# One decoder step on one core: squares taken in pairs, key groups and weight splits moved, and each chunk's products run one accumulator bank after the other

## The reference, cut to what matters

```python
def rmsnorm(x, g):
    xf = x.astype(jnp.float32)
    y = xf * lax.rsqrt(jnp.mean(xf * xf, axis=-1, keepdims=True) + EPS)
    return (y * g.astype(jnp.float32)).astype(x.dtype)

def ffn_half(x, g_pre, g_post, wi, wo):
    return x + 0.5 * rmsnorm(swiglu(rmsnorm(x, g_pre), wi, wo), g_post)

for i in range(DEPTH):                       # DEPTH = 2, D_MODEL = 1024, D_FF = 2816
    xp = ffn_half(xp, g[0], g[1], ffn1_wi[i], ffn1_wo[i])
    hp = rmsnorm(xp, g[2])
    yp = ab_mixer(hp, ...) if i % 2 == 0 else c_mixer(hp, ...)
    xp = xp + rmsnorm(yp, g[3])
    xp = ffn_half(xp, g[4], g[5], ffn2_wi[i], ffn2_wo[i])
    xp = xp + (p_prompt[i] @ ple_w_pe[i]) * jax.nn.sigmoid(rmsnorm(xp, g[6]) @ ple_w_pg[i])
```

## Time and profile before

| What | Value |
|---|---|
| Runs | 2132.02 us, median of 3 (2131.34 to 2139.12) |
| The profiled execution | 2124.92 us; its span in the trace 2123.1 us |
| TensorE busy | 2094.1 us (99%), 17060 products |
| VectorE, ScalarE, GpSimd busy | 1133.2 us (53%), 712.7 us (34%), 33.5 us (2%) |
| Granted TensorE clock, mean | 0.997 of 2.4 GHz |
| Chain that ended last | PE 85%, DVE 10%, ACT 2% |

### The profile page before, as it was taken

One profiled execution on the slowest core, in us unless ns is written; L12 is line 12 of the kernel. 1 busy time (PEld: TensorE's weight loads), 2 busy tenths in 40 slices (PEclk: granted clock), 3 DMA queues, 4 the chain that ended last, 5 costly groups with the idle time before them and its releaser, 6 DMA issues.

```text
span 2123.1 us, 37973 instructions
## 1 busy us (share of the span) xinstructions
PE 2094.1 (99%) x17060; PEld 2057.1 (97%) x17060; DVE 1133.2 (53%) x1545; ACT 712.7 (34%) x926; POOL 33.5 (2%) x68
## 2 busy tenths in 40 slices
PE   8999999999999999999999999999999999999998
PEld 8999999998879999999999999999998999999998
DVE  6433244855766754234587343244888854323467
ACT  5221122422344422112354222123477432212243
POOL 0000000011010000000000000000000000000000
PEclk9999999999999999999999999999999999999999
DMA  5222222233132222222232222222222132232222
GB/s 173 95 82 87 98 97 80 81 121 120 60 121 80 80 100 90 91 100 82 79 108 100 80 97 88 95 100 80 79 84 101 60 120 83 87 100 90 100 90 81
DMA packets 33633, 198.57 MB, mean 94 GB/s; under 512 B 4648, under 2 KB 4936, under 8 KB 15552
## 3 DMA queue, kind: packets, MB, share of 16 engines
q1 hardware_dynamic: 29520, 183.87, 24.7%
q0 software_dynamic: 3952, 12.28, 1.7%
HBM read 191.68 MB, written 4.46 MB: 92 GB/s over the span
## 4 chain that ended last, share of the span: by engine, by line
PE 85%; DVE 10%; ACT 2%; issue 1%; DMA 1%; POOLq 0%; DVEq 0%; POOL 0%; ACTq 0%
PE acc L1729 69%; PE acc L1834 9%; DVE w_lo L1022 2%; DVE t L1135 2%; PE acc L1770 1%; DVE x L1142 1%; DVE act_lo L1148 1%; PE acc L2034 1%; DVE rs_post L1130 1%; PE acc L2104 1%; DVE xsum L1157 1%; PE acc L1914 1%; DMA raw<-in_weights 1%; PE acc L1968 1%; PE acc L1989 1%
## 5 line engine op out<-in xcount | busy, mean ns | idle before, releaser
L1729 PE MATMUL acc<-act_hi,w_hi 128*128 128x260 f32 x3072 | 621.6, 284 | 0.0
L1729 PE MATMUL acc<-act_hi,w_lo 128*128 128x260 f32 x3072 | 617.5, 282 | 0.0
L1729 PE MATMUL acc<-act_lo,w_hi 128*128 128x260 f32 x3072 | 617.0, 282 | 0.0
L1729 PEld LDWEIGHTS acc<-act_hi,w_hi 128*128 128x128 f32 x3072 | 472.6, 188 | 1.7 <-issue 1.0
L1729 PEld LDWEIGHTS acc<-act_hi,w_lo 128*128 128x128 f32 x3072 | 472.3, 188 | 0.4
L1729 PEld LDWEIGHTS acc<-act_lo,w_hi 128*128 128x128 f32 x3072 | 471.6, 188 | 0.5
L620 ACT ACTIVATE w_hi<-raw 128x2048 fp32r<-128x2048 f32 (+2 forms) x179 | 323.8, 1809 | 277.0 <-DMA raw<-in_weights 276.9
L1022 DVE TENSOR_TENSOR w_lo<-raw,w_hi 128x2048 fp32r<-128x2048 f32 (+2 forms) x179 | 387.6, 2165 | 43.0 <-ACT w_hi L620 42.8
L1267 DVE TENSOR_TENSOR gu<-acc,rs_pre 128x520 f32<-128x520 f32 x164 | 114.3, 698 | 439.4 <-PE acc L1729 439.3
L745 ACT ACTIVATE hid_hi<-gu 128x520 fp32r<-128x520 f32 x86 | 55.0, 639 | 476.5 <-DVE gu L1287 476.5
L1729 PE MATMUL acc<-hid_hi,w_hi 128*128 128x260 f32 x1024 | 206.3, 283 | 0.2
(11 more groups left out here) (287 smaller groups left out, 2148.5 us busy)
## 6 DMA issues: line engine op xcount, KB each, us to landing
raw<-in_weights SPq DMA_DIRECT2D x138, 1024.0 KB, 4.8
raw<-in_weights SPq DMA_DIRECT2D x32, 896.0 KB, 4.6
ring<-in_k_pages POOLq DMA_DIRECT2D x16, 256.0 KB, 4.7
ring<-in_v_pages POOLq DMA_DIRECT2D x16, 256.0 KB, 3.6
raw<-in_weights SPq DMA_DIRECT2D x12, 256.0 KB, 5.3
x<-in_x SPq DMA_DIRECT2D x8, 260.0 KB, 6.6
out_y<-x SPq DMA_DIRECT2D x8, 260.0 KB, 2.0
raw<-in_weights SPq DMA_DIRECT2D x4, 512.0 KB, 3.4
```

Of the source, the lines that this page charges most:

```text
L1729: ins = nc.tensor.matmul(a[0:width, half, 0:HALF], w[slot][:, at:at + width], m[:, half * HALF:(half + 1) * HALF], start=first and n == 0, ...
```

## The change

Four edits. (1) `chunk` runs the three products of one half, all into one bank, and then the three of the other half; the low weights come second instead of third. (2) In `begin`, the squares of two chunks are one instruction of 520 columns and added as such, with one add at the end that folds the two sides (`fold_sum`); VectorE's reciprocal for `pre0` and the drain behind it stand one chunk earlier, the drain of `first1.0` one chunk later, and ScalarE takes the root of `pre0` ahead of its half-1 parts. (3) In the attention, key groups 1, 2 and 3 stand in tiles c0, c1 and c2 (before: v3, x0 and c1), the rows of values behind c0 (before: inside the first head's scores), `decay_sums` at head 2 (before: head 1), and the last head's transposes inside tile b3. (4) In the recurrence, the splits at `i5` and `i7` stand earlier, and the weights of the last output pair (`HALVED`) are split and waited for in two halves.

```diff
 def head_jobs(h):
-    return [["c0", "dec_s2", "x0"], ["dec_s3", "c1", "x1"], ["c2", "x2", "dec_t"], ["dec_p", "c3", "dec_o0", "x3"],
-            ["dec_o1", "b0"], ["dec_o2", "b1"], ["dec_o3", "b2"], ["b3"]][h]
+    return [["dec_s1", "c0", "vt0", "vt2", "x0"], ["dec_s2", "c1", "x1"], ["dec_s3", "c2", "x2", "dec_t"], ["dec_p", "c3", "dec_o0", "x3"],
+            ["dec_o1", "b0"], ["dec_o2", "b1"], ["dec_o3", "b2"], ["pt7.0", "pt7.2", "b3"]][h]
...
+HALVED = PLAN.unit[f"{S_C}.out6"]
...
+                    at = 0
+                    if n == HALVED:
+
+                        at = size // 2
+                        nc.scalar.activation(w_hi[n % SLOTS][:, 0:at], raw(n, at), ACT.Copy).then_inc(half_hi, 1)
...
-                for c in range(KC):
-                    square_half(s, 0, c)
-                    if c == 4:
+                for n in range(4):
+                    square_two(s, 0, n)
+                    if n == 2:
                         root(f"{s}.post1", rs_post, 1)
                 done(f"{s}.first0.0")
+                root(f"{s}.pre0", rs_pre, 0)
                 for c in range(KC):
                     high_half(s, 1, c)
-                    if c == 2:
-                        root(f"{s}.pre0", rs_pre, 0)
...
                 roots(range(0, 4))
+                done(f"{s}.i5")
                 gelus(range(0, 4))
-                done(f"{s}.i5")
...
+            def add_two(s, half, n):
+
+                dve.wait_ge(xsq_ready, square_count(s, 4 * half + n))
+                if n > 1:
+                    dve.wait_ge(xsum_added, added_count(s, 4 * half + n - 1))
+                nc.vector.tensor_tensor(xsum[:, :], xsum[:, :], pair_square(n)[:, :], ALU.add).then_inc(xsum_added, 1)
+
+            def fold_sum(s, half):
+
+                dve.wait_ge(xsum_added, added_count(s, 4 * half + 3))
+                nc.vector.tensor_tensor(cols(xsum, 0), cols(xsum, 0), cols(xsum, 1), ALU.add).then_inc(xsum_added, 1)
...
-                    if c == 3:
+                    if c == 2:
                         invert(f"{s}.pre0", rs_pre, 0)
                         if s == S_AB + 1:
                             dve.wait_ge(stored, 16 * 5)
                         first_drain(s, 0, 0)
-                    if c == 5:
+                    if c == 6:
                         first_drain(s, 1, 0)
...
-                    if h == 1:
+                    if h == 2:
                         decay_sums()
-                    if h == 2:
                         decode_softmax()
...
                 for c in range(4):
                     mixed(c)
+                done(f"{s}.i7")
                 gates(7)
                 mixed_lo(0)
                 mixed_lo(1)
-                done(f"{s}.i7")
...
-                for n, (w, m) in enumerate(((w_hi, hi), (w_hi, lo), (w_lo, hi))):
-                    for half in range(2):
+                for half in range(2):
+                    for n, (w, m) in enumerate(((w_hi, hi), (w_lo, hi), (w_hi, lo))):
...
-                wait_unit(unit)
+                if unit == HALVED:
+                    pe.wait_ge(half_lo, 1)
+                else:
+                    wait_unit(unit)
                 accs = claim(J[name])
                 for c in range(KC):
+                    if unit == HALVED and c == KC // 2:
+                        wait_unit(unit)
...
                     for m in B_TILES.get(h, []):
-                        column_tile(f"b{m}", f"b{m // 2 * 2}", m % 2, with_values(h - 3) if h < MIX_HEAD else None)
+                        column_tile(f"b{m}", f"b{m // 2 * 2}", m % 2, with_values(h - 3) if h < MIX_HEAD else
+                                    lambda c: transposes(MIX_HEAD) if c == 5 else None)
```

More of the change, by code:

```diff
@@ L218, in ab @@
             pl.add_job(f"{s}.v{m}", f"{s}.v{m}")
-            pl.add_job(f"{s}.dec_s{m // 2}")
+            if m == 0:
+                pl.add_job(f"{s}.dec_s0")
             pl.add_job(f"{s}.v{m + 1}", f"{s}.v{m}")
-        for j in ("cq", "ck0", "s0.0", "vt0", "s0.2", "vt2"):
+        for j in ("cq", "ck0", "s0.0", "s0.2"):
             pl.add_job(f"{s}.{j}")
@@ L405, in both, with pair_square @@
             return cols(ap, half).unsqueeze(1).broadcast_to([P, 2, HALF])
-        def half_square(half, c):
-            return cols(xsum, half) if c == 0 else cols(xsq[c // 2 % 2], c % 2)
+        def pair_square(n):
+            return xsum if n == 0 else xsq[n % 2]
         def acc_of(name):
@@ L492, in act_count, with square_count, added_count @@
             return sum(2 * KC if n % 4 else KC for n in range(s)) + KC * half + c + 1
-        def added_count(s, half, c):
-            return sum(2 * (KC - 1) if n % 4 else KC - 1 for n in range(s)) + (KC - 1) * half + c
+        def square_count(s, n):
+            return KC * s + n + 1
+        def added_count(s, n):
+            return sum(KC if i % 4 else KC - 1 for i in range(s)) + n
         def ysum_count(s, n):
@@ L678, in high_half, with square_two @@
                                      scale=pre_gain(s, c)).then_inc(acth_ready, 1)
-            def square_half(s, half, c):
-                if c > 4:
-                    act.wait_ge(xsum_added, added_count(s, half, c - 4))
-                elif half and c:
-                    act.wait_ge(xsum_added, added_count(s, 0, KC - 1))
-                nc.scalar.activation(half_square(half, c), cols(x[:, c, :], half), ACT.Square).then_inc(xsq_ready, 1)
+            def square_two(s, half, n):
+                if n == 3:
+                    act.wait_ge(xsum_added, added_count(s, 4 * half + 1))
+                elif half and n:
+                    act.wait_ge(xsum_added, added_count(s, 4))
+                nc.scalar.activation(two(pair_square(n)[:, :]), half_of(x[:, 2 * n:2 * n + 2, :], half), ACT.Square)\
+                    .then_inc(xsq_ready, 1)
             def first_taps(s, c):
@@ L722, in begin @@
                     nc.scalar.activation(p_hi[:, :, :], p_raw[:, :, :], ACT.Copy).then_inc(ph_ready, 1)
-                for c in range(KC):
-                    square_half(s, 1, c)
+                for n in range(4):
+                    square_two(s, 1, n)
                 root(f"{s}.pre1", rs_pre, 1)
@@ L1223, in begin @@
                 done(f"{s - 1}.out67.1")
-                for c in range(1, 4):
-                    add_half(s, 0, c)
+                for n in range(1, 3):
+                    add_two(s, 0, n)
                 invert(f"{s}.post1", rs_post, 1)
-                for c in range(4, KC):
-                    add_half(s, 0, c)
+                add_two(s, 0, 3)
+                fold_sum(s, 0)
                 done(f"{s}.first0.0")
@@ L1248, in begin @@
                 first_drain(s, 2, 0)
-                for c in range(1, KC):
-                    add_half(s, 1, c)
+                for n in range(1, 4):
+                    add_two(s, 1, n)
+                fold_sum(s, 1)
                 if s % 4 == 3:
@@ L2063, in decode_probs, with transposes @@
                     ins.then_inc(acc_ready, 1)
+                def transposes(h):
+                    pe.wait_ge(probs_ready, QB * (h + 1))
+                    for kb in range(QB):
+                        if kb % 2 == 0:
+                            a = claim(J[f"{s}.pt{h}.{kb}"])
+                        for qb in range(kb, QB):
+                            ins = nc.tensor.transpose(a[:, kb % 2, qb * P:(qb + 1) * P],
+                                                      sc[:, qb, kb * P:(kb + 1) * P], ident)
+                        if kb % 2:
+                            ins.then_inc(acc_ready, 1)
                 decay_column()
```

74 lines of the change are left out of this document (34 added, 40 removed).

## The result

The changed kernel takes 2116.9 us (median of 6 runs, 2114.6 to 2119.6) against 2130.7 us for before (6 runs, 2124.4 to 2139.1): ratio 0.9933, 95% interval 0.9913 to 0.9953, 0.7% less. The two profiled executions, 2124.92 and 2116.38 us, lie 8.5 us apart, the very sum of the prediction. That is luck: its terms are off by up to 2 us each and cancel, and the medians lie 13.8 us apart. Both have to be explained.

What follows compares the result with a forecast made beforehand. TensorE bounds the kernel, busy 2094.1 of 2123.1 us: its product pace and its waits. Terms +2.0 - 4.3 - 2.0 - 5.1 + 1.3 - 0.4 = -8.5 us off the median 2132.02 gave 2123.5; own range 2118 to 2128, overall 2098 to 2139.

Steps and rivals of the forecast that it cites:

- edit 1, order: `chunk`: weights change more often over 12,288 products, costing 2.0 us; adds into one bank taken as no effect.
- edit 2, six begins: `begin`: 1.64 us of TensorE waiting becomes 0.92, a gain of 0.7, six times: 4.3 us.
- edit 4, recurrence: Last output pair: halves shorten the 1.9 us wait for `w_lo`, gain 2.0 us; moved splits at `i5` and `i7` gain 0.
- edit 3, waits: Attention: `decay_sums` at head 2 loses 1.3 us; around b3 1.4 gained, 1.0 lost, net 0.4 gained.
- edit 3, clock: Attention, first heads: the 10.24 us stretch at 1.2 GHz goes, gaining 5.1 us.
- Every sign that the prediction named: Whole trace: slightly under 1672 products from 100 to 300 us; clock 1.00 in first heads; third-head scores wait over 1 us.
- first two rivals: `chunk`, 8,192 products: bank changes cost, new order saves 2.8 ns each (0.27); or adds into one bank cost 3 ns (0.13).
- three priced waits: Attention: third head's scores wait 1.3 us more, claim ahead of b3 loses 1.0, last transposes gain 1.4 of 1.6.
- third rival: Attention: waits only move and the clock falls all the same, sum -3.4 us, time 2128.6 us; chance 0.18.

Runs made afterwards that it cites:

- after_banks6_weights5: The kernel after with another order in `chunk`: banks alternate at every product, weights change at 5 of 6; median 2119.8 us, ratio 0.9956 to before.
- only_attention: The kernel before with edit 3 alone (the attention's part of the diff); median 2121.5 us, ratio 0.9973.
- only_begin: The kernel before with edit 2 alone (squares in pairs, order of adds, reciprocal and drains in the six begins); median 2122.4 us, ratio 0.9976.
- only_recurrence: The kernel before with edit 4 alone (last output unit split in halves, splits at `i5` and `i7` moved); median 2122.6 us, ratio 0.9977.

## Why the prediction was right and wrong

| Term | predicted, us | measured alone, net us |
| --- | --- | --- |
| edit 1, order | +2.0 | +3.0 +- 0.5 (pace: +3.3) |
| edit 2, six begins | -4.3 | -5.1 +- 0.5 |
| edit 4, recurrence | -2.0 | -1.8 +- 0.5 |
| edit 3, waits | +0.9 | -1.1 +- 0.5 |
| edit 3, clock | -5.1 | -4.7 +- 0.8 (loss 10.2 to 5.5) |
| sum | -8.5 | -9.7 |

The four net terms sum to -5.0 us; after as a whole has 5.2 less than before (2112.0 against 2117.2). So the edits add up, and no large part comes from their standing together. Every sign that the prediction named came: 1670 products from 100 to 300 us, the waits in `begin` and at the last output pair, the clock in the first heads, the longer wait in the third head.

**The base is the step that failed.** The prediction took 8.5 us off a median of three runs, 2132.0, and kept the 7.1 us by which it stood above the profile. Over 62 runs the median of before is 2128.4: 3.6 of the 6.6 us by which the forecast was high. And those 7.1 us were not a thing around the kernel that stays. The clocks of those three runs are not on record, but in the 62 it is clock loss that sets the longer runs apart, the very thing that edit 3 was costed to remove once. The change took 5 us of it from the mean run; six runs of it lie 5 us apart, where the six of before beside them lie 15 apart.

**Edit 1**: right that banks bring no great effect (the first two rivals, 2.8 and 3 ns on 8,192 products, fall: no order lies more than 0.61 ns from another). Mis-sized: two thirds of `half_pair`'s difference gave 0.16 ns a product; it was 0.27. Two readings are off. Four of six products had the weights of the one before, not three, so the share is three quarters. And the difference of 0.24 ns is too small: by the starts in the trace of before `half_pair` begins a product every 120.01 ns on `act` and 120.12 on `hid`, 0.42 and 0.21 more than `chunk`. Three quarters of these are 3.4 us, by this estimate. The agreement with 3.3 does not show that the weights are all, since after_banks6_weights5 is slower on `act` than `half_pair`.

The Trainium skill, page "TensorE: Matmul & The Clock Gate", section "A second HAM failure mode: psum-queue depth-cycling", tells of a kernel that cycles through banks and whose clock swings between the two levels; after_banks6_weights5 alternates two banks at each product and stays at 1.00 from 100 to 300 us, so that is not seen here.

**Edit 2**: right in mechanism and to 0.1 us in each time of VectorE's chain. Missed was what came with it, the 0.87 us of the mean: in the first of the six begins it started 0.54 us late, waiting for `xsum`, and the product behind it 0.11 late; in the fifth, 0.23 us were lost in the same two places. After has none of these. Whether the wider squares or the new order of VectorE's work gave the gain was not tried apart.

**Edit 4**: right, with the moves worth nothing within the error.

**Edit 3**: the three priced waits came as priced. The scores wait 1.4 more (1.3 predicted), the claim of b3 1.25 (1.0), and the last transposes wait 0.30 in place of 1.72 (1.4 gained). The last two in after:

```profile
619.88 0.36 PE L1751 MATMUL acc<-act_hi,w_hi 128*128 128x260 f32 x1 [1.09 <-DVE sc L1464]
...
627.08 2.34 PE L2138 MATMUL acc<-pt,v_tok 128*64 128x512 f32 x8
```

What was not counted is a gain: in all five traces with the old attention TensorE waits 0.5 to 1.0 us for pages of keys in v3, in three of them 0.5 for the first values, and in the profiles of after and only_attention no such wait is left. Together these leave about +0.2 us, and the two profiles agree within 0.3 (-3.20 in the attention, of which -5.1 and +1.7 are the clock). The net times of only_attention say -1.1 +- 0.5; the steps of the recorded clock are large enough for the rest, but that is not shown. The third rival (the clock falls all the same) is half true: it falls in the third head, for less.

The Trainium skill, the same page, section "HAM oscillation — how this bites in real kernels", tells of waits for DMA data that bring the clock down. The falls at 544.47 and 1623.08 us in after also stand behind waits (from 540.7 and 1620.4 us), though these are for ScalarE's results. By 480 us the trace of before shows another kind, since hardly anything waited ahead of it (9.81 of 10.14 us busy); what brought it is open:

```profile
470.00:480.14 10.14, 9.81 (x80) 1.00 0.10 16
```

**The new wait for `sig`** (+1.39) can't be tied to any edit. It follows a load of 1 MB for the last embedding, issued 5.5 us ahead of the first product of that tile in all 14 profiled executions, that landed 7.7 us after its issue in after; ScalarE's split, a table load and the sigmoids stand behind it, and TensorE waits for these:

```profile
2087.95 1.92 ACT L633 ACTIVATE w_hi<-raw 128x2048 fp32r<-128x2048 f32 x1 [7.74 <-DMA raw<-in_weights]
2089.88 1.28 ACT L999 ACT_TABLE_LOAD   x1
...
2092.94 0.36 PE L1751 MATMUL acc<-act_hi,w_hi 128*128 128x260 f32 x1 [1.25 <-DVE sig L1136]
```

In before the same split starts 0.2 us behind that product (2096.02 against 2095.82), in after 2.2. In the 14 it starts between 0.8 us ahead and 2.2 behind, and all five with 1.4 or more, two of them kernels with one edit alone (only_begin and only_recurrence), have this wait, of 0.6 to 1.4 us. Without it the two profiles would lie 9.9 us apart.

## What to carry to other kernels

Before one profile is taken for a kernel, look at the clock of several runs: a difference of a few us may be the stretch at 1.2 GHz that this execution had or hadn't, and a term that removes such a stretch is priced by its mean loss over runs, not by one trace. Taking each run's clock loss off its time shows effects of 1 us in a kernel whose runs spread over 20. And a sum that comes out right proves little: here terms that were off by up to 2 us met by cancelling, and only kernels with one edit showed it.

## What the runs showed of the hardware that was not expected

- The same program on one chip ran with a mean granted clock between 0.989 and 0.999 (62 runs); in the profiles of kernels with the old attention the stretch at 1.2 GHz in the first heads lasted from nothing to 20.48 us.
- A fall of the clock between two waits cost little: of 3.41 us at 1.2 GHz at 1623 us in after, which lose 1.7, the wait behind them gave back 1.5 (2.41 to 0.89 us).
- The pace of products of 260 columns, one behind the other at full clock, depends on the order of weights and banks by up to 0.6 ns of 120, and differently for `act` and `hid`.
- The same load of 1 MB at the same place took 4.7 to 7.7 us from issue to landing (14 profiled executions).
